# Stick-breaking attention on Trainium2: each 128x128 transpose taken as two transposes of 64 rows

## The reference, cut to what matters

```python
def one_block(args):
    q_blk, blk = args
    t_pos = blk * Q_BLOCK + jnp.arange(Q_BLOCK)
    mask = key_pos[None, :] < t_pos[:, None]
    z = jnp.einsum('bhqd,bhkd->bhqk', q_blk, k).astype(jnp.float32) * scale
    log_nb_raw = jax.nn.log_sigmoid(-z)
    log_b = z + log_nb_raw
    log_nb = jnp.where(mask, log_nb_raw, 0.0)
    excl = lax.cumsum(log_nb, axis=3, reverse=True) - log_nb
    a = jnp.where(mask, jnp.exp(log_b + excl), 0.0)
    return jnp.einsum('bhqk,bhkd->bhqd', a.astype(v.dtype), v)
```

## Time and profile before

| | |
|---|---|
| time, median of 3 runs | 4849.63 us (4846.13 to 4852.17) |
| time of the profiled execution | 4848.74 us |
| its span on the core | 4846.9 us |
| granted TensorE clock, mean of the span | 0.972 |
| attention, from its first scan to its last | 1162.85 to 2675.91 us |

### The profile page before, as it was taken

How to read it: one execution, slowest core, us unless ns; L and a number is a source line. 1 busy time by engine, 2 the same in 40 slices (tenths; PEclk the granted TensorE clock), 3 DMA queues, 4 the chain that set the end, 5 groups by cost and what they waited for, 6 DMA issues and landing times. The chain is left out here.

```text
span 4846.9 us, 76501 instructions
## 1 busy us (share of the span) xinstructions
PE 4538.5 (94%) x24271; PEld 3347.9 (69%) x24273; DVE 2905.4 (60%) x3384; ACT 2659.9 (55%) x3994; POOL 624.5 (13%) x771
## 2 busy tenths in 40 slices
PE   7999979996999999999999799956999999999998
PEld 5777857774555555555556588845777878888776
DVE  3222246667887887888888333356666555555665
ACT  3222234445777777777777332222676666665665
POOL 0000001221000000000000000021333332232233
PEclk9999999998999999999999899978999999999999
DMA  3222231113002001001000433332666555555663
GB/s 131 100 100 100 78 102 52 60 44 111 14 30 64 14 27 54 27 27 40 23 5 6 151 137 125 137 133 89 235 229 216 207 202 202 199 188 187 232 236 140
DMA packets 279535, 539.37 MB, mean 111 GB/s; under 512 B 38320, under 2 KB 103856, under 8 KB 279344
## 3 DMA queue, kind: packets, MB, share of 16 engines
q1 hardware_dynamic: 228512, 410.49, 24.1%
q0 software_dynamic: 46224, 118.03, 7.2%
q10 hardware_dynamic: 4608, 8.39, 0.5%
HBM read 410.97 MB, written 176.16 MB: 121 GB/s over the span
## 5 line engine op out<-in xcount | busy, mean ns | idle before, releaser
L940 DVE TENSOR_TENSOR_SCAN att_R<-att_stay,att_R 128x512 f32<-128x512 f32 x896 | 1070.7, 1264 | 126.2 <-ACT att_stay L881 86.6
L891 ACT ACTIVATE att_RT<-att_rt 128x512 f32<-128x512 f32 (+3 forms) x1152 | 586.4, 562 | 283.6 <-PE att_rt L833 252.1
L833 PEld LDWEIGHTS att_rt<-ident,att_R 128*128 128x128 f32 x4224 | 454.1, 141 | 318.0 <-issue 187.8
L833 PE MATMUL att_rt<-ident,att_R 128*128 128x128 f32 x4224 | 590.5, 280 | 23.0 <-ACT att_RT L891 14.5
L881 ACT ACTIVATE att_stay<-att_z 128x1024 f32<-128x1024 f32 (+2 forms) x576 | 552.9, 960 | 104.7 <-PE att_z L815 52.2
L845 PE MATMUL att_out<-att_RT,att_dv 128*64 128x512 f32 (+3 forms) x2304 | 518.0, 570 | 0.0
L1252 DVE TENSOR_TENSOR ew_lo<-ew_raw,ew_hi 128x1024 fp32r<-128x1024 f32 x372 | 430.4, 1221 | 10.1 <-ACT ew_hi L1245 10.1
L1245 ACT ACTIVATE ew_hi<-ew_raw 128x1024 fp32r<-128x1024 f32 x384 | 373.7, 1050 | 0.0
L243 PE MATMUL qkv_out<-qkv_u_hi,qkv_w_hi 128*128 128x512 f32 x768 | 309.8, 403 | 19.2 <-DVE qkv_u_lo L234 19.2
L243 PE MATMUL qkv_out<-qkv_u_hi,qkv_w_lo 128*128 128x512 f32 x768 | 303.2, 395 | 0.0
L243 PE MATMUL qkv_out<-qkv_u_lo,qkv_w_hi 128*128 128x512 f32 x768 | 301.2, 392 | 0.0
(11 more groups left out here) (263 smaller groups left out, 8366.2 us busy)
## 6 DMA issues: line engine op xcount, KB each, us to landing
ew_raw<-in_w_e_gate SPq DMA_DIRECT2D x32, 2048.0 KB, 9.7
ew_raw<-in_w_e_up SPq DMA_DIRECT2D x32, 2048.0 KB, 10.2
ew_raw<-in_w_e_down SPq DMA_DIRECT2D x32, 2048.0 KB, 9.7
qkv_x<-in_x SPq DMA_DIRECT2D x32, 512.0 KB, 5.0
lru_x<-in_x SPq DMA_DIRECT2D x32, 512.0 KB, 5.1
mix_raw<-s_mix_t SPq DMA_DIRECT2D x32, 512.0 KB, 4.2
mix_x<-in_x SPq DMA_DIRECT2D x32, 512.0 KB, 4.8
s_h<-mix_h SPq DMA_DIRECT2D x32, 512.0 KB, 3.6
```

The source lines that it names most:

```text
L833: last = nc.tensor.transpose(rt[h][:, qt * P:(qt + 1) * P], R[:, n % 3, h, qt, s * P:(s + 1) * P], k.ident[:])
L891: nc.scalar.activation(RT[:, h, s, queries], rt[h][:, queries], ACT.Copy).then_inc(rt_copied[h], 1)
L940: nc.vector.tensor_tensor_scan(R[:, n % 3, h, s, 0:width][:, ::-1], src[:, ::-1], src[:, ::-1], initial, ALU.mult, ALU.bypass).then_inc(sc ...
```

## The change

The block of R that was transposed in one instruction of 128 rows (queries) and 128 columns (keys) is transposed in two instructions of 64 rows each: `half` 0 takes queries 0 to 63 of the tile from partitions 0 to 63, `half` 1 the others. The moving operand is the 64x64 corner of the identity that belongs to the half. The results of half 0 go to one PSUM buffer and those of half 1 to the other, for both heads; before, a buffer belonged to a head. The loop order is head, tile of queries, half, so the two halves follow each other directly. `turned` copies a half at a time and puts the queries back in order in `RT` by writing pieces of 64 elements. `transposes` now waits once for all 8 scans of the unit and for both copies of the step before, with three `hold`s, where it had four waits hung on instructions; `rt_done` of both halves comes with the last two transposes of a step, where that of head 0 came in the middle. `scans` waits for both before its first scan. `values` reads `RT` by another name for the same elements.

```diff
@@ attention
-        RT = sb("att_RT", [P, 2, 4, GT])
+        RT = sb("att_RT", [P, 2, 4, TT, 2, HD])
-        rt = [ps(f"att_rt{i}", [P, GT]) for i in range(2)]
+        rt = [ps(f"att_rt{half}", [P, 2, TT, HD]) for half in range(2)]
@@ def transposes(pe, hp, step):
             n = step // 4
+            hold(pe, k, scanned, 8 + hp * 8 * U + 8 * n + 8)
+            for half in range(2):
+                hold(pe, k, rt_copied[half], hp * K + step + 1)
             for h in range(2):
-                pe.wait_ge(scanned, 8 + hp * 8 * U + 8 * n + 7 + h)
-                pe.wait_ge(rt_copied[h], hp * K + step + 1)
                 for qt in range(query_start(c, G, s) // P, TT):
-                    last = nc.tensor.transpose(rt[h][:, qt * P:(qt + 1) * P], R[:, n % 3, h, qt, s * P:(s + 1) * P],
-                                               k.ident[:])
-                last.then_inc(rt_done[h], 1)
+                    for half in range(2):
+                        lanes = slice(half * HD, (half + 1) * HD)
+                        last = nc.tensor.transpose(rt[half][:, h, qt, :], R[lanes, n % 3, h, qt, s * P:(s + 1) * P],
+                                                   k.ident[lanes, lanes])
+                        if h == 1 and qt == TT - 1:
+                            last.then_inc(rt_done[half], 1)
@@ def values(pe, hp, step):
-                                        RT[:, h, s, queries], start=(c == G and s == 0), stop=(c == 0 and s == 3))
+                                        RT[:, h, s].rearrange("p t half q -> p (t half q)")[:, queries], start=(c == G and s == 0), stop=(c == 0 and s == 3))
@@ def turned(act, hp, step):
-            for h in range(2):
-                act.wait_ge(rt_done[h], 12 + hp * K + step + 1)
-                if h == 0:
+            first = query_start(c, G, s) // P
+            for half in range(2):
+                act.wait_ge(rt_done[half], 12 + hp * K + step + 1)
+                if half == 0:
                     act.wait_ge(av_done, hp * K + step + 1)
-                nc.scalar.activation(RT[:, h, s, queries], rt[h][:, queries], ACT.Copy).then_inc(rt_copied[h], 1)
+                nc.scalar.activation(RT[:, :, s, first:, half, :], rt[half][:, :, first:, :], ACT.Copy).then_inc(rt_copied[half], 1)
@@ def scans(dve, hp, step):
+            for half in range(2):
+                dve.wait_ge(rt_done[half], hp * K + 4 * n + 4)
             for h in range(2):
-                dve.wait_ge(rt_done[h], hp * K + 4 * n + 4)
```

More of the change, by code:

```diff
@@ L885, in turned @@
             G, c, s = unit_of(step)
-            queries = slice(query_start(c, G, s), GT)
-            for h in range(2):
-                act.wait_ge(rt_done[h], 12 + hp * K + step + 1)
-                if h == 0:
+            first = query_start(c, G, s) // P
+            for half in range(2):
+                act.wait_ge(rt_done[half], 12 + hp * K + step + 1)
+                if half == 0:
                     act.wait_ge(av_done, hp * K + step + 1)
-                nc.scalar.activation(RT[:, h, s, queries], rt[h][:, queries], ACT.Copy).then_inc(rt_copied[h], 1)
+                nc.scalar.activation(RT[:, :, s, first:, half, :], rt[half][:, :, first:, :], ACT.Copy).then_inc(rt_copied[half], 1)
         def results(act, hp, step):
```

## The result

The changed kernel takes 4681.1 us (median of 4 runs, 4678.79 to 4684.18) against 4850.5 before: a ratio of 0.9653, 95% interval 0.9641 to 0.9665. 4676 was forecast. The profiled execution's span fell from 4846.9 to 4679.2 us. All of it is in attention: from the first scan to the last values product it took 2686.2 - 1162.9 = 1523.3 us before and 2515.2 - 1161.6 = 1353.6 now, 169.7 less.

The account below looks back on a forecast made before the run. PE was taken to bound attention, with DVE the bound afterwards. Full units 1055, diagonal units 256, loop 14 and handover waits 15 make 1340 us against 1513, 173 less: 4676 us, range 4640 to 4725 (0.63).

Parts of the forecast that it names:

- What bounds before: Attention before the change: PE is full, 5.52 us a pair of steps; DVE would stop it at 4.71.
- The transposes: PE's transposes: a pair of halves takes 0.06 us, a step 0.48 in place of 0.87; 0.78 less a pair of steps.
- The handovers: PE between transposes and scores: the cost of changing between 128 and 64 rows goes, 0.32 us less a pair of steps.
- PE's pace: PE in full units after the change: 4.42 us a pair of steps, 8.84 a unit.
- VectorE as the new bound: Full units of attention: VectorE (DVE) sets the pace at 4.71 us a pair of steps, 9.42 a unit.
- The diagonal units: 32 diagonal units: 6.0 us of scans plus 2.0 of starving each, 256 us; PE's own need 7.3 us each.
- The loop: Three changes of head pair in attention: 14 us with the refill.
- Waits at handovers: DVE's waits because PE has only 0.3 us of slack a pair: 0.13 us a unit, 15 us.
- The pair gains nothing on PE: Rival on transposes: a pair takes about 0.11 us, only handovers saved, 72 us, 4778; 0.23 for both PE-side rivals.
- slower: Rival on transposes: halves pay full price in turn or can't be fed, up to 5240; 0.10 together with dearer copies.
- the copies become the bound: Rival on ACT's copies: pieces of 64 cost 80% more, 0.88 us a copy; within the 0.10 for a slower kernel.
- The holds cost a stop at each step: Rival on PE's waits: near 0.35 us a step, only 77 us less, 4773; 0.23 for both PE-side rivals.

Follow-up runs that it names:

- before_copy: Kernel before the change with each scan replaced by a plain copy on VectorE (running product left out): 4850.6 us, ratio 0.9995.
- after_same_rows: Changed kernel with both transposes of a pair taken from partitions 0 to 63, so they can't overlap: 4845.0 us, ratio 0.9983.
- after_copy_wide: Changed kernel with copies for scans, plus one product of 128 rows and one column ahead of each pair of score steps: 4690.5 us, ratio 0.9666.
- after_copy: Changed kernel with each scan replaced by a plain copy on VectorE (running product left out): 4635.6 us, ratio 0.9557.
- lead10: Changed kernel with scores ten steps ahead of the values in place of eight, and six stay buffers in place of four: 4647.8 us, ratio 0.9582.
- lead10_unrolled: Changed kernel with scores ten steps ahead, six stay buffers and the loop over head pairs written out: 4612.7 us, ratio 0.9510.
- after_unrolled: Changed kernel with attention's loop over head pairs written out on TensorE, ScalarE and VectorE: 4651.2 us, ratio 0.9589.
- before_holds: Kernel before the change with only the new waits, three holds at the head of each step: 4859.6 us, ratio 1.0017.

## Why the prediction was right

*What bounds before.* Right, and more so than I wrote: `before_copy` moved nothing.

*The transposes.* A pair of halves was forecast at 0.06 us. Sixteen in 0.71 us, of which 0.22 are the length of the last and 0.05 the first one's wait for its weights, make (0.71 - 0.22 - 0.05) / 7 = 0.063 for each of the seven pairs behind the first. Loads and products of both halves overlap; `after_same_rows` is the proof, with the whole gain lost. Rows of another product (the scores) were the right place to read it from. The bound without overlap, 0.12 a pair, was right too: 2 x 0.062 there. The Trainium skill (TensorE: Matmul & The Clock Gate, LDWEIGHTS) puts a load at its columns over 1.2 per nanosecond, an estimated 107 ns for 128 of them; the measurement disagrees for these loads, since they start 0.062 us apart in `after_same_rows`, where they follow each other on the same rows.

*The handovers.* 0.32 us a pair of steps was forecast; the rows give 0.16 - 0.02 ahead of the scores (0.52 - 8 x 0.062 = 0.02 is left) and 0.22 - 0.09 behind them, 0.27. The term was a little too large. `after_copy_wide` bounds it from above: there two changes of shape and a small product cost 0.22 us together.

*PE's pace.* 4.42 us forecast, 4.48 found. *VectorE as the new bound.* Right, at 9.41 us a unit; `after_copy` shows 8.97 behind it, and that the margin is only 5%.

*The diagonal units.* 2.0 us of loss each was forecast. A diagonal unit takes 8.31 us in the loop against 6.0, so 2.3, and 0.4 more in the unit behind it where that is a full one. Cause and place were right, as `lead10` shows. The size is 0.7 short at most. The 6.0 itself was a little high, since in `lead10_unrolled`, where nothing starves, the shortest diagonal units take 5.72. But PE's own cost of it, 7.3 us, was wrong: 9.0. As the rows have it, that is because I left the writing out of results on ScalarE out of the walk.

*The loop.* 14 us was taken for the changes of head pair. `after_unrolled` gives 22 for all that the loop costs, in which the waits on registers are. About 10 of them stand at the two changes: the two units behind each take 12.85 + 10.10 and 13.57 + 10.93 us in place of 4 x 9.41. The rest is spread over the diagonal units.

*Waits at handovers.* 15 us was taken, and nearly none are there in full units away from the diagonals and the loop's turn: 9.41 throughout. One reading under it was off: the second copy ends 1.08 - 0.60 = 0.48 us behind the first, and not 0.55. Added up by kind, the 112 full units take 1070 us, loop and waits included, where 1055 + 14 + 15 = 1084 were forecast, and the 32 diagonal ones 270, where it was 256: 14 us too much in the one and 14 too little in the other. In all 1340 us were forecast from the first scan to the last; 2501.4 - 1161.6 = 1339.8 were found. That VectorE becomes the bound, and at what pace, was worked out; that the sum hits to the microsecond is luck.

*The rivals.* "The pair gains nothing on PE", "slower" and "the copies become the bound" are out, by the rows after. "The holds cost a stop at each step" is out as it was put (`before_holds`: 8 us in all), but there is something in it: 0.15 us for each one behind a late semaphore. The changed kernel stands just at the edge where they begin to cost.

## What to carry to other kernels

Where half of the array's rows is enough for an operation, try two halves that use different rows: here they ran as two streams on TensorE, and the gain could be read beforehand from another 64-row product in the trace, the scores. Before costing such a gain, find the next engine's floor from a stretch in which it had work in store, not from its mean busy share: here that floor took a fifth of it (0.22 of 1.03 us a pair of steps). When the bound has moved, look at where the new one starves, here at the short units, and give it more in store ahead of them.

## What was not expected of the hardware

- The two halves of the rows need not alternate in the program: with eight transposes of one half and then eight of the other, a product of the one started 0.06 to 0.18 us ahead of three earlier-listed ones of the other, and two thirds of the gain stayed (4737 against 4681 and 4850 us).
- A wait in an instruction of its own on TensorE cost 0.15 us each where it stood behind one that was met late, and nothing where there was time for it: three more at each step, 150 us; three, or the one that plain waits leave, the same 8.97 us a unit.
- Full scans that wait for nothing start 1.18 us apart whatever TensorE does beside them (1.178 before the change, 1.177 after).
- Writing out a loop of three turns on three engines saved 22 us of attention and, for no reason that I can show, 9 us of the stages behind it, in both kernels where it was tried.
